# Ten expert tiles instead of six ahead of the expert stage, a ring of twelve slots, and x gathered as plain float32

## The reference

```
def expert_choice_moe(x, router_w, w1, w3, w2):
    cap = EC_CAPACITY_FACTOR * s // N_EXPERTS             # 64 tokens for each of 16 experts
    aff = softmax(einsum('bsd,de->bse', x, router_w))
    gates, idx = lax.top_k(aff.transpose(0, 2, 1), cap)
    xg = vmap(lambda xb, ib: xb[ib])(x, idx)              # each expert's 64 tokens
    hid = silu(einsum('becd,edf->becf', xg, w1)) * einsum('becd,edf->becf', xg, w3)
    ye = einsum('becf,efd->becd', hid, w2) * gates[..., None]
    return scatter-add of ye to the tokens idx
...
    ple = sigmoid(x @ ple_gate_w[i] + ple_gate_b[i]) * (p[i] @ ple_w[i])
    x = layer_norm(DEEPNORM_ALPHA * x + ffn + ple, ln2_g[i], ln2_b[i])
```

## Time and profile before

| | us |
|---|---|
| median of three runs (3446.2 to 3449.67) | 3448.42 |
| span of the profiled execution | 3446.9 |
| TensorE busy in it | 3242.4 |
| VectorE busy | 1296.3 |
| ScalarE busy | 958.9 |

### The profile page before, as it was taken

One profiled execution on the slowest core, in us unless ns is written; L12 is line 12 of the kernel. 1 busy time (PEld: TensorE's weight loads), 2 busy tenths in 40 slices (PEclk: granted clock), 3 DMA queues, 4 the chain that ended last, 5 costly groups with the idle time before them and its releaser, 6 DMA issues. The chain is left out here.

```text
span 3446.9 us, 39641 instructions
## 1 busy us (share of the span) xinstructions
PE 3242.4 (94%) x15918; PEld 2176.3 (63%) x15918; DVE 1296.3 (38%) x1781; ACT 958.9 (28%) x1570; POOL 238.9 (7%) x377
## 2 busy tenths in 40 slices
PE   7999999999999999999997999999988999999996
PEld 5885578887787567888785466444436556544442
DVE  4315554242522564333366472111116656111112
ACT  3325433132322533323242431000004543000001
POOL 1004200000101410000000200000000320000000
PEclk9999999999999999999997999999999999999999
DMA  5410122321540022222311216999992112799997
GB/s 156 129 43 24 64 87 94 98 93 57 137 127 32 1 86 86 98 92 92 89 36 23 86 56 257 422 424 424 424 417 75 61 62 93 304 423 424 424 424 303
DMA packets 234149, 590.12 MB, mean 171 GB/s; under 512 B 42690, under 2 KB 146184, under 8 KB 184852
## 3 DMA queue, kind: packets, MB, share of 16 engines
q1 hardware_dynamic: 234004, 588.08, 45.1%
HBM read 581.75 MB, written 2.10 MB: 169 GB/s over the span
## 5 line engine op out<-in xcount | busy, mean ns | idle before, releaser
L2579 PE MATMUL ps<-w_ring,xe 128*64 128x512 f32 x1024 | 235.9, 604 | 5.0 <-PEq L119 5.0
L422 DVE TENSOR_TENSOR mlp_w_lo<-w_ring,mlp_w_hi 128x2048 fp32r<-128x2048 f32 x62 | 142.1, 2292 | 212.7 <-ACT mlp_w_hi L382 212.7
L357 PE MATMUL ps<-h_hi,in_w_hi 128*128 128x512 f32 (+1 forms) x528 | 207.0, 392 | 2.1 <-DVE h_lo L430 2.1
L357 PE MATMUL ps<-h_hi,in_w_lo 128*128 128x512 f32 (+1 forms) x528 | 205.6, 389 | 0.0
L357 PE MATMUL ps<-h_lo,in_w_hi 128*128 128x512 f32 (+1 forms) x528 | 205.6, 389 | 0.0
L357 PE MATMUL ps<-h_hi,mlp_w_hi 128*128 128x512 f32 x512 | 202.6, 396 | 2.1 <-DVE h_lo L430 2.1
L357 PE MATMUL ps<-h_hi,mlp_w_lo 128*128 128x512 f32 x512 | 202.5, 396 | 0.0
L357 PE MATMUL ps<-h_lo,mlp_w_hi 128*128 128x512 f32 x512 | 202.5, 395 | 0.0
L357 PE MATMUL ps<-mlp_w_hi,u_lo 128*128 128x512 f32 x512 | 202.3, 395 | 0.0
L357 PE MATMUL ps<-mlp_w_hi,u_hi 128*128 128x512 f32 x512 | 202.2, 395 | 0.0
L357 PE MATMUL ps<-mlp_w_lo,u_hi 128*128 128x512 f32 x512 | 202.2, 395 | 0.0
(11 more groups left out here) (560 smaller groups left out, 6480.5 us busy)
## 6 DMA issues: line engine op xcount, KB each, us to landing
w_ring<-in_w SPq DMA_DIRECT2D x192, 1024.0 KB, 12.4
ex_front<-in_w SPq DMA_DIRECT2D x96, 1024.0 KB, 12.8
ex_back<-in_w SPq DMA_DIRECT2D x96, 1024.0 KB, 13.0
w_ring<-in_w_in SPq DMA_DIRECT2D x32, 1024.0 KB, 5.4
w_ring<-in_w_up SPq DMA_DIRECT2D x32, 1024.0 KB, 5.5
w_ring<-in_w_down SPq DMA_DIRECT2D x32, 1024.0 KB, 5.0
w_ring<-in_cmp_w SPq DMA_DIRECT2D x16, 512.0 KB, 5.0
w_ring<-in_w_out SPq DMA_DIRECT2D x8, 1024.0 KB, 6.0
```

The costliest lines, as they stand in the source:

```text
L357: mm = pe.matmul(ps[0:o.rows, bank[k], 0:o.cols], lhsT, rhs, start=(o.first and j == 0), stop=(o.final and j == len(o.mm) - 1))
L422: dve.tensor_tensor(w.lo[:, home(n), 0:used], ring.slots[:, n % RING, 0:used], w.hi[:, home(n), 0:used].bitcast(F32), ALU.subtract).then_i ...
L2579: mm = pe.matmul(ps[rows, bank + half, :], lhsT, slot(2 * m + a)[:, kk, 512 * half:512 * half + 512], start=(k == 0), stop=(k == DC - 1))
```

## The change

More tiles are fetched ahead: `AHEAD` goes from 2 to 6, so ten tiles (4 in the weight ring, 6 in `front`) are fetched in the routing stage, all eight of w1 and the first two of w3; `back` keeps 2 slots, and the ring has 12 slots instead of 8. x is kept once, as plain float32, instead of as a pair, and the scratch area for GpSimd's DMAs is set to 1 KB when the program is made. With x in one part, `gather` has 32 plain float32 products instead of 64 products of parts; the selection and the affinities are plain float32 too. The order of tiles, the arithmetic of an expert and the number of turns stay. The fetch in the loop addresses its tile by one row number instead of an expert and a range of rows; the DMA has the same shape as before (128 rows of 8 KB).

```
@@ route_beside
         for m in range(AHEAD):
             dst = E.front[:, m, :].rearrange("p (k n) -> p k n", k=2)
-            sp.dma_start(dst, expert_rows(E.w1, RING + m)).then_inc(E.ready[m], 16)
+            sp.dma_start(dst, expert_rows(E.order, RING + m)).then_inc(E.ready[m], 16)
...
-        pool.tensor_copy(E.aff_now.hi[:, :, :], aff_s.hi[:, :, 0:2]).then_inc(s.staged, 1)
-        pool.tensor_copy(E.aff_now.lo[:, :, :], aff_s.lo[:, :, 0:2]).then_inc(s.staged, 1)
+        pool.tensor_copy(E.aff_now[:, :, :], aff_s[:, :, 0:2]).then_inc(s.staged, 1)
...
-    def round_x(act, s):
+    def keep_x(act, s):
         for t in range(TT):
-            act.activation(xs.hi[:, t, :], x[:, t, :], ACT.Copy).then_inc(s.x_hi, 1)
+            act.activation(xs[:, t, :], x[:, t, :], ACT.Copy).then_inc(s.x_kept, 1)
...
-        for t in range(TT):
-            dve.wait_ge(s.x_hi, t + 1)
-            dve.tensor_tensor(xs.lo[:, t, :], x[:, t, :], xs.hi[:, t, :].bitcast(F32), ALU.subtract).then_inc(s.x_lo, 1)
...
-        c.link(dve.tensor_copy(aff_s.hi[:, :, :], aff[:, :, :]))
-        c.link(dve.tensor_tensor(aff_s.lo[:, :, :], aff[:, :, :], aff_s.hi[:, :, :].bitcast(F32), ALU.subtract))
...
-AHEAD = 2
-def expert_rows(w1, n):
-    return w1[n % 2][256 * (n // 2):256 * (n // 2) + 256, :].rearrange("(p k) n -> p k n", k=2)
+AHEAD, BACK = 6, 2
+def expert_rows(order, n):
+    w, q, a = order[n // 8], n // 2 % 4, n % 2
+    return w[a][256 * q:256 * q + 256, :].rearrange("(p k) n -> p k n", k=2)
...
 def gather(pe, ps, bank, xs, E, j):
     for t in range(TT):
-        for part in (xs.hi, xs.lo):
-            mm = pe.matmul(ps[:, bank + j // 4, j % 4 * P:j % 4 * P + P], part[:, t, pairs_of(j)], E.sel_now[:, t, :],
-                           start=(t == 0 and part is xs.hi), stop=(t == TT - 1 and part is xs.lo))
+        mm = pe.matmul(ps[:, bank + j // 4, j % 4 * P:j % 4 * P + P], xs[:, t, pairs_of(j)], E.sel_now[:, t, :], start=(t == 0), stop=(t == TT - 1))
...
@@ experts
-        back = sb("ex_back", [P, RING - AHEAD, SLOT])
+        back = sb("ex_back", [P, BACK, SLOT])
...
-        slots = 2 * RING
+        slots = RING + AHEAD + BACK
...
-                    src = w[bass.ds(2 * it + a, 1), 256 * q:256 * q + 256, :].rearrange("o (p k) n -> p (o k) n", p=P)
+                    row = (2 * it + a) * D + 256 * q
+                    src = w.rearrange("e r n -> (e r) n")[bass.ds(row, 256), :].rearrange("(p k) n -> p k n", p=P)
...
-                        for part in (aff_now.hi, aff_now.lo):
-                            mm = pe.matmul(ps[:, TR_BANK + 1, 0:2], sel_now[:, t, :], part[:, t, :],
-                                           start=(t == 0 and part is aff_now.hi), stop=(t == TT - 1 and part is aff_now.lo))
+                        mm = pe.matmul(ps[:, TR_BANK + 1, 0:2], sel_now[:, t, :], aff_now[:, t, :], start=(t == 0), stop=(t == TT - 1))
...
-    nc = bacc.Bacc("TRN2", target_bir_lowering=False, num_devices=1)
+    nc = bacc.Bacc("TRN2", target_bir_lowering=False, num_devices=1, dynamic_dma_scratch_size=1024)
```

More of the change, by code:

```diff
@@ L2202, in sb @@
         return ctx.enter_context(sbuf(nc, f"{name}{i}", shape, F32))
-    rw, lg, aff = sb("rw", [P, DC, NE]), sb("lg", [P, TT, NE]), sb("aff", [P, TT, NE])
+    rw, lg, aff = sb("rw", [P, DC, NE]), sb("lg", [P, TT, NE]), aff_s
     mx, work, top = sb("mx", [P, 3, TT]), sb("work", [NE, 2, T]), sb("top", [NE, 8, 8])
@@ L2270, in go @@
                 pe.wait_ge(s.selected, 1)
-                pe.wait_ge(s.x_lo, TT)
+                pe.wait_ge(s.x_kept, TT)
             for j in range(4 * b, 4 * b + 4):
@@ L2355, in rest_of_p, with x_is_kept, expert_tiles @@
             dve.tensor_tensor(pT.lo[:, j, :], ps[:, ROUTE_A + j, :], pT.hi[:, j, :].bitcast(F32), ALU.subtract).then_inc(s.p_lo, 1)
-    def x_is_split(dve, s):
-        dve.wait_ge(s.x_lo, TT)
-    names = ("rw_in iota_in pt_in pb_in ones x_hi x_lo rw_hi rw_split by_expert taken logits softmax less_max exped aff_done "
+    def x_is_kept(dve, s):
+        dve.wait_ge(s.x_kept, TT)
+    names = ("rw_in iota_in pt_in pb_in ones x_kept rw_hi rw_split by_expert taken logits softmax less_max exped aff_done "
              "aff_flipped top places placed back pos_done p_flipped p_hi p_lo staged selected gathered xe_done")
     return beside(names, sp, {0: bias_in, 1: logits_by_expert, 2: logits_by_token, 4: affinities_by_expert, 11: places_by_token, 13: p_by_feature, 16: p_ready, 18: gather_half(0), 20: gather_half(1)},
-                  {0: round_x, 3: exponentials, 14: round_p, 20: take_half(0), 22: take_half(1)},
-                  {0: split_router, 1: softmax, 3: take_top(0, 3), 4: take_top(3, 8), 7: places, 11: keep_places, 14: rest_of_p, 15: select_first, 16: x_is_split}, pool)
-AHEAD = 2
-def expert_rows(w1, n):
-    return w1[n % 2][256 * (n // 2):256 * (n // 2) + 256, :].rearrange("(p k) n -> p k n", k=2)
+                  {0: keep_x, 3: exponentials, 14: round_p, 20: take_half(0), 22: take_half(1)},
+                  {0: split_router, 1: softmax, 3: take_top(0, 3), 4: take_top(3, 8), 7: places, 11: keep_places, 14: rest_of_p, 15: select_first, 16: x_is_kept}, pool)
+AHEAD, BACK = 6, 2
+def expert_rows(order, n):
+    w, q, a = order[n // 8], n // 2 % 4, n % 2
+    return w[a][256 * q:256 * q + 256, :].rearrange("(p k) n -> p k n", k=2)
 def pairs_of(k):
     return slice(256 * (k // 2) + k % 2, 256 * (k // 2) + k % 2 + 255, 2)
-def expert_tiles(w1):
-    return [tile(2, D, lambda slot, n=n: [(slot, expert_rows(w1, n))], None) for n in range(RING)]
+def expert_tiles(order):
+    return [tile(2, D, lambda slot, n=n: [(slot, expert_rows(order, n))], None) for n in range(RING)]
 def select(dve, E, iota):
@@ L2499, in stage_affinities @@
                 def stage_affinities(it):
-                    pool.tensor_copy(aff_now.hi[:, :, :], aff_s.hi[:, :, bass.ds(2 * it, 2)]).then_inc(s.aff_staged, 1)
-                    pool.tensor_copy(aff_now.lo[:, :, :], aff_s.lo[:, :, bass.ds(2 * it, 2)]).then_inc(s.aff_staged, 1)
+                    pool.tensor_copy(aff_now[:, :, :], aff_s[:, :, bass.ds(2 * it, 2)]).then_inc(s.aff_staged, 1)
                 def turn(it):
@@ L2526, in flip_selection @@
                     for t in range(TT):
-                        mm = pe.transpose(ps[:, TR_BANK, t * P:(t + 1) * P], sel_now[:, t, :].bitcast(F32), C.ident[:, :])
+                        mm = pe.transpose(ps[:, TR_BANK, t * P:(t + 1) * P], sel_now[:, t, :], C.ident[:, :])
                     mm.then_inc(s.sel_flipped, 1)
                     if not first(it):
-                        pe.wait_ge(s.aff_staged, it * 2)
+                        pe.wait_ge(s.aff_staged, it)
                     for t in range(TT):
-                        for part in (aff_now.hi, aff_now.lo):
-                            mm = pe.matmul(ps[:, TR_BANK + 1, 0:2], sel_now[:, t, :], part[:, t, :],
-                                           start=(t == 0 and part is aff_now.hi), stop=(t == TT - 1 and part is aff_now.lo))
+                        mm = pe.matmul(ps[:, TR_BANK + 1, 0:2], sel_now[:, t, :], aff_now[:, t, :], start=(t == 0), stop=(t == TT - 1))
                     mm.then_inc(s.weighed, 1)
@@ L2751, in sb @@
             return c.enter_context(sbuf(nc, f"{name}{i}", shape, F32))
-        xs = pair(nc, ctx, f"xs{i}", [P, TT, D])
+        xs = sb("xs", [P, TT, D])
         front, xe, pt = sb("ex_front", [P, AHEAD, SLOT]), sb("xe", [P, 2, DC, CAP]), sb("p", [P, TT, PLE])
-        iota, pos, aff_s = sb("iota", [P, CAP]), sb("posd", [P, TT, NE]), pair(nc, ctx, f"affs{i}", [P, TT, NE])
-        pos_now, aff_now = sb("pos_now", [P, 2 * TT, 2])[:, 0:TT, :], pair(nc, ctx, f"aff_now{i}", [P, TT, 2])
-        sel_now = ctx.enter_context(sbuf(nc, f"sel_now{i}", [P, TT, P], F32R))
+        iota, pos, aff_s = sb("iota", [P, CAP]), sb("posd", [P, TT, NE]), sb("affs", [P, TT, NE])
+        pos_now, aff_now = sb("pos_now", [P, 2 * TT, 2])[:, 0:TT, :], sb("aff_now", [P, 2 * TT, 2])[:, 0:TT, :]
+        sel_now = sb("sel_now", [P, TT, P])
         E = Names(front=front, xe=xe, sel_now=sel_now, pos_now=pos_now, aff_now=aff_now,
-                  ready=[ctx.enter_context(nc.semaphore(f"ex{i}_ready{n}")) for n in range(RING)], w1=I["w1_2"][i])
+                  ready=[ctx.enter_context(nc.semaphore(f"ex{i}_ready{n}")) for n in range(AHEAD + BACK)], order=[I[n][i] for n in ("w1_2", "w3_2", "w2_2")])
         with ExitStack() as c2:
@@ L2765, in block2_layer @@
             side = route_beside(nc, c2, ps, C, x, xT, pt, pT, pb, I, iota, pos, aff_s, xs, E, i)
-            gemm(nc, f"pl{i}", ps, ring, ple, RING, expert_tiles(I["w1_2"][i]),
+            gemm(nc, f"pl{i}", ps, ring, ple, RING, expert_tiles(E.order),
                  flips(C, lambda i, j: x[:, i, j * P:(j + 1) * P], xT, halves=True), side=side, banks=ROUTE_A)
```

## The result

| | before | after |
|---|---|---|
| median of the runs, us | 3447.98 | 3420.66 (3414.67 to 3421.58) |
| ratio, with its 95% interval | | 0.9921 [0.9906, 0.9936] |
| span of the profiled execution, us | 3446.9 | 3419.6 |
| expert stage, layer 0: first product to end of last | 468.1 | 455.6 |
| expert stage, layer 1 | 468.4 | 455.6 |

A forecast was written before the change was run, and what follows sets the result against it. Transfers were taken to bound the expert stage, with TensorE close behind. Tiles ahead -19.8 and routing stage +3.0 summed to -16.8 us, taking the median from 3448.4 to 3431.6 us; range 3425 to 3443 us.

The forecast's parts named there:

- the part on the tiles ahead: Expert stages: with four more tiles ahead, the last tile lands 9.9 us earlier a layer, 19.8 us in both.
- The fetch itself has the same shape, so 2.472 us stays: Expert-stage transfers: time per 1 MiB tile was to stay at 2.472 us.
- lower end: Whole kernel: 3425 us, as nothing in the rows was said to give more than 19.8 + 1.2 us.
- three things that were to show it wrong: Gather record over 0.145 us; expert-stage DMA share well under 1; no TensorE tile wait at layer's end with stage over 459 us.
- queue that is full from the first release: Expert stage: transfers assumed without pause until the last tile, giving 9.9 us a layer.
- the third rival, no gain: Expert stage: transfers pause in the first turns with a full ring, tiles ahead gain nothing; 3451.4 us, chance 0.05.
- Their cover in the routing stage: Routing stage: four extra tiles take 9.9 us of 28 us of idle DMA before p, so they cost nothing.
- The gather: Between w3 and w2: 64 records at 0.135 us, 8.6 us, 0.9 more; covered by transfers in the expert stage.
- Both rivals on the gather: Passes and loads add up: 0.176 us a record, 3467.8 us, chance 0.08; half size: 0.150 us, 3442.2 us, chance 0.09.
- The routing stage: Gather for the first two experts, uncovered: 0.9 us plus 0.6 for changing over a layer, 3.0 us in all.
- the 0.3 us per change: Routing stage: price of changing over between products of parts and a plain product; two halves make 0.6 us a layer.
- TensorE's waits: Expert stage: waits on tiles were to fall from 18.9 to some 3 us a layer, left in the last turns.

The follow-up runs named there:

- e5: Changed kernel with its twelve slots, but only two of front's six tiles fetched early, so six tiles ahead; ratio to the kernel before 0.9976.
- e8: Changed kernel, but SyncE issues the expert stage's first tile only when TensorE has done six of the ten tiles; ratio to the kernel before 1.0002.
- e10: Changed kernel with three empty pads, so all twelve slots begin on multiples of 256 bytes; ratio to the kernel before 0.9899.
- e4: Changed kernel with x allocated ahead of the weight ring, moving the ring's four slots up by 16 KB; ratio to the kernel before 0.9902.
- e7: Changed kernel with AHEAD, BACK = 4, 0: eight tiles ahead in eight slots; ratio to the kernel before 0.9989.
- e9: Kernel before with three empty pads of 128 bytes, so all eight slots begin on multiples of 256 bytes; ratio to the kernel before 0.9980.

## Why the prediction was wrong, step by step

**The step that failed is in the part on the tiles ahead: "The fetch itself has the same shape, so 2.472 us stays".** The shape did stay. What changed is where the tiles land: two of eight slots on a multiple of 256 bytes became six of twelve, because `AHEAD` sets the size of `front` and `front` happens to lie on one. A tile then takes 2.457 us (58.97 / 24) instead of 2.472, and over 182 tiles that is 2.7 us a layer, 5.3 in both. The prediction had 0. Its lower end, "nothing in the rows gives more than 19.8 + 1.2 us", rested on the same sentence; without this term the gain would have been 22 us, inside the range. None of the three things that were to show it wrong came (a record of the gather takes 0.121 us, the DMA share is 1.01, TensorE waits 1.3 us for the last tiles); the 59.3 us a turn that it expected is what failed.

**The tiles ahead themselves: right, in mechanism and size.** From e5 to the changed kernel the stages go from 464.7 to 455.6 and from 464.6 to 455.6 us, 9.1 and 9.0 a layer against 9.9 said. But e5 differs in one thing more than the four early tiles. At the start of a stage it issues six fetches; the changed kernel, like the kernel before, issues two and the next only when TensorE has reported its first tiles. Windows of 3 us behind those first fetches, before, after and in e5 (columns as in the earlier trace rows):

```profile
2118.00:2121.00 3.00, 3.00 (x16) 1.09 (x14) 0.00 (x0) 0.00 (x0) 0.00 (x0) 1.00 0.97 320
```

```profile
2118.00:2121.00 3.00, 3.00 (x16) 1.10 (x14) 0.00 (x0) 0.00 (x0) 0.00 (x0) 1.00 0.95 306
```

```profile
2124.00:2127.00 3.00, 3.00 (x18) 1.09 (x15) 0.00 (x0) 0.00 (x0) 0.00 (x0) 1.00 1.03 434
```

At 306 to 320 GB/s instead of 427 about 0.8 us of transfer are missing, before and after alike, and none in e5. So the four tiles are worth 9.1 + 0.8 = 9.9 us a layer by e5, or 4 x 2.457 = 9.8 by the tile, 19.7 in both; and of the 3.4 and 3.8 us by which e5's stages are shorter than those of the kernel before, 0.8 belong to this pause and the rest is the rate. The "queue that is full from the first release" was not quite so, but the pause stands on both sides of the comparison. Behind it the ring didn't run dry (DMA share 1.01 from the early turns to the late ones), so the third rival, no gain, is out. e8 is the counter-proof: transfers that begin 12.3 and 12.4 us late make stages that are 12.5 and 11.8 us longer.

**Their cover in the routing stage: right.** SyncE issues the six tiles in one go, and windows of DMA share show them gone before p is asked for. The timeline of SyncE after, then the windows:

```profile
2020.71 3.73 SPq L2216 DMA_DIRECT2D ex_front<-in_w  x6
2065.01 0.38 SPq L2218 DMA_DIRECT2D p<-in_p  x1
```

```profile
2020.00:2038.00 18.00, 15.26 (x68) 10.07 (x67) 10.02 (x16) 12.54 (x17) 0.00 (x0) 0.80 0.91 356
2038.00:2044.00 6.00, 6.00 (x29) 4.71 (x28) 1.95 (x7) 0.26 (x1) 0.00 (x0) 1.00 0.00 0
2044.00:2060.00 16.00, 16.00 (x64) 10.55 (x63) 12.21 (x23) 5.01 (x5) 0.00 (x0) 1.00 0.01 2
```

They have landed by 2038 (the prediction said before 2040), 27 us ahead of p, which is issued where it was the earlier trace rows.

**The gather: over-priced by 0.9 us.** A record of a plain product costs 7.73 / 64 = 0.121 us, what a record of parts cost, not the 0.135 read from the earlier trace rows. Those eight records stand between products of another kind: in the trace the first starts 0.21 us ahead of the second and the last 0.21 us ahead of the next kind, and between them they start 0.112 us apart, so their 1.08 us hold two dear ends. So two products of parts and one plain product have one price at this shape. By the rule of four passes (the Trainium skill, FP8 and Floating Point Precision, TensorE Precision Notes) the gather was to take, by the prediction's estimates, 7.0 us under hidden loads and 11.3 if passes and loads add up; at 7.73 both are off. Both rivals on the gather, with 0.176 and 0.150 us a record, are out.

**The routing stage: +3.0 said, 0.0 measured.** The issue of the router's weights and the first fetch of the expert stage in the timeline of SyncE, layer 0, before and after:

```profile
2019.22 0.37 SPq L2211 DMA_DIRECT2D rw<-in_router_w  x1
...
2112.36 0.81 SPq L2470 DMA_DIRECT2D ex_back<-in_w  x2
```

```profile
2019.35 0.37 SPq L2211 DMA_DIRECT2D rw<-in_router_w  x1
...
2112.51 0.80 SPq L2464 DMA_DIRECT2D ex_back<-in_w  x2
```

93.14 and 93.16 us. No record is dearer, and no price of a change of kind shows: half a gather there takes 3.68 us with the step to the next product, and took 3.73. What the 0.3 us per change worked out from the earlier trace rows were, was not tried; that row's plain product has 512 moving columns and two rows, not the gather's shape.

**TensorE's waits: 8 us left a layer, not 3.** The prediction let the dearer gather eat spare time and set the transfers only 2.7 us behind; without those 6.3 us its own sum leaves 458.5 - 449.5 = 9.0 us, near the 8.3 and 8.1 measured.

**The tails: 2.0 us that no step had.** Behind the last expert product come 16 products of the scatter. The windows of the 6 us that follow that product in layer 1, before, after and in e10 (the same columns; in each of these three TensorE is busy for 19.27 of the 23.55 us up to it, at a granted clock of 1.00):

```profile
3420.41:3426.46 6.05, 3.46 (x10) 2.69 (x9) 3.21 (x4) 1.79 (x2) 0.00 (x0) 0.73 0.00 0
```

```profile
3394.13:3400.18 6.05, 3.46 (x16) 2.82 (x16) 3.80 (x6) 2.36 (x4) 0.00 (x0) 1.00 0.00 0
```

```profile
3390.59:3396.60 6.01, 3.42 (x10) 2.68 (x10) 3.28 (x4) 1.86 (x2) 0.00 (x0) 0.74 0.00 0
```

Where the granted clock is 1.00 all 16 products start in that time, where it is 0.73 or 0.74 only ten: part of them ran at the lower level of 1.2 GHz. In the kernel before the clock falls 2.8 us behind the last expert product, after a wait of 2.6 us in which TensorE was idle; in the changed kernel it falls only 8.7 us behind it, when the 16 products are done. In both layers the changed kernel, e4, e7 and e9 have the quick tail (25.4 to 25.5 us in layer 1) and all the others a slower one (25.7 to 26.5). e9 has nothing of the change, and e10 has all of it. So the 2.0 us are in the profile of the changed kernel, but the change by itself doesn't decide them; what does stays open, and so does whether the runs without a profile share it.

**The sum against the measurement.** Tiles ahead -19.7, slots on the multiple -5.3, routing 0.0, tails -2.0: -27.0 us of the 27.3. Said were -19.8, 0, +3.0 and 0. The one large gain came out as said, and all three errors pointed the same way.

## What to carry to other kernels

Where transfers bound a stage, look at where their destination begins before you call two fetches alike: here slots that all begin 128 or 192 bytes past a multiple of 256 cost 1.3 to 1.4% of the rate against slots that all begin on one, and a pad of 128 bytes made the difference. A buffer whose size changes can move others onto or off such a boundary, or, as here, hold more of the slots that lie on one, so an edit's own gain is known only with the places held fixed, as e5 holds them. And price an operation from a row that stands in a long run of its own kind: the eight records between others read as 0.135 us, where the gather's 64 came to 0.121.

## What the runs showed that was not expected

The rate of the transfers goes with the share of slots on a multiple, but not slot by slot. Two windows of about two tiles each in the changed kernel:

```profile
3246.49:3251.41 4.92, 4.38 (x22) 1.38 (x18) 0.00 (x0) 0.00 (x0) 0.00 (x0) 1.00 1.01 421
3251.41:3256.32 4.91, 3.61 (x18) 1.27 (x16) 0.00 (x0) 0.00 (x0) 0.00 (x0) 1.00 1.01 427
```

Of the six pairs of tiles that make a cycle of its ring one goes at 417 to 421 GB/s and the others at 427 to 429, although three pairs lie off a multiple; and half of the slots on the multiple give 58.97 us where all give 58.87 and none 59.69. Why tiles on the multiple help the ones behind them was not tried and stays open.
